# Two-layer decoder trunk: value products by fours, layer 0's first rows normed two by two, one product of its end moved back

## The reference

```python
for i in range(2):
    x = x + mixer_i(rms_norm(x, norm_i)) @ w_out_i
return rms_norm(x, final_norm)

# mixer 0: sliding window of 128, 4 key/value groups, partial rope, a sink logit per head
q, k, v, gate = split(h @ w_in)
o = banded_attention(rope(q), rope(k), v, 127, sinks);   return o * silu(gate)

# mixer 1: three patterns (window, dilation) = (128,1), (512,4), (2048,16), each with own q, k, v
for gi: o_gi, lse_gi = banded_attention on every dil-th row
w = softmax over gi of lse_gi;   return sum(w_gi * o_gi) * silu(gate)
```

## Time and profile before

| | us |
|---|---|
| median of 3 runs | 1302.64 (1300.87 to 1304.35) |
| profiled execution, its own time | 1303.58 |
| its span | 1301.8 |
| granted TensorE clock, mean | 0.995 |
| PE busy | 1261.5 (97%) |
| PE weight load busy | 1184.5 (91%) |
| DVE busy | 768.7 (59%) |
| ACT busy | 644.3 (49%) |
| POOL busy | 370.1 (28%) |

### The profile page before, as it was taken

One profiled execution on the slowest core, in us unless ns is written; L12 is line 12 of the kernel. 1 busy time (PEld: TensorE's weight loads), 2 busy tenths in 40 slices (PEclk: granted clock), 3 DMA queues, 4 the chain that ended last, 5 costly groups with the idle time before them and its releaser, 6 DMA issues.

```text
span 1301.8 us, 24575 instructions
## 1 busy us (share of the span) xinstructions
PE 1261.5 (97%) x8714; PEld 1184.5 (91%) x8714; DVE 768.7 (59%) x2339; ACT 644.3 (49%) x1777; POOL 370.1 (28%) x427
## 2 busy tenths in 40 slices
PE   4999999999899999999999999999999999999997
PEld 4999998988799999999989999999999899987997
DVE  5745453555662545666646776556765566768925
ACT  6445463545741445554546555446554456546312
POOL 2312151240401022212212942215922217710110
PEclk9999999999999999999999999999999999999999
DMA  5101022031546211110121321202211212314723
GB/s 203 35 24 50 26 60 79 18 98 49 159 151 202 96 27 54 39 27 19 33 74 50 92 67 27 74 26 67 84 58 36 65 38 80 92 36 127 223 98 129
DMA packets 101223, 97.29 MB, mean 75 GB/s; under 512 B 30704, under 2 KB 87536, under 8 KB 101104
## 3 DMA queue, kind: packets, MB, share of 16 engines
q1 hardware_dynamic: 101104, 95.73, 24.6%
HBM read 79.46 MB, written 16.25 MB: 74 GB/s over the span
## 4 chain that ended last, share of the span: by engine, by line
PE 80%; issue 5%; DVE 4%; DMA 4%; POOL 3%; ACT 2%; SPq 1%; DVEq 0%; POOLq 0%; ACTq 0%
PE j_bank L1196 56%; PE o_bank L1339 6%; PE t_bank L1318 5%; PE s_bank L1305 4%; PE j_bank L1283 3%; PE s_bank L1307 2%; POOL xr L1129 1%; DMA w_raw<-in_w_qkv 1%; DMA coef<-coef_dram 1%; PE o_bank L1196 1%; PE t_bank L1196 1%; DMA gate<-in_positions 1%; PE s_bank L1196 1%; DVE xr L1843 1%; POOL xr L1136 1%
## 5 line engine op out<-in xcount | busy, mean ns | idle before, releaser
L1196 PE MATMUL j_bank<-w_hi,ht_hi 128*128 128x384 f32 (+1 forms) x1312 | 445.0, 339 | 4.2 <-ACT v L1452 2.4
L1196 PE MATMUL j_bank<-w_lo,ht_hi 128*128 128x384 f32 (+1 forms) x1312 | 432.9, 330 | 0.0
L1196 PE MATMUL j_bank<-w_hi,ht_lo 128*128 128x384 f32 (+1 forms) x1312 | 432.8, 330 | 0.0
L1196 PEld LDWEIGHTS j_bank<-w_hi,ht_hi 128*128 128x128 f32 x1312 | 248.5, 189 | 15.0 <-issue 7.9
L1438 ACT ACTIVATE probs<-probs,stat 128x256 f32<-128x256 f32 (+1 forms) x512 | 231.1, 453 | 58.8 <-DVE stat L1697 56.8
L1090 POOL TENSOR_TENSOR w_lo<-w_raw,w_hi 128x768 fp32r<-128x768 f32 (+1 forms) x60 | 104.2, 1736 | 543.6 <-ACT w_hi L1429 444.0
L1196 PEld LDWEIGHTS j_bank<-w_lo,ht_hi 128*128 128x128 f32 x1312 | 248.8, 190 | 0.0
L1196 PEld LDWEIGHTS j_bank<-w_hi,ht_lo 128*128 128x128 f32 x1312 | 248.4, 189 | 0.0
L1429 ACT ACTIVATE w_hi<-w_raw 128x768 fp32r<-128x768 f32 (+1 forms) x120 | 88.4, 763 | 83.3 <-PE j_bank L1196 43.6
L826 ACT COPY probs_t<-t_bank 128x256 f32<-128x256 f32 (+1 forms) x84 | 39.0, 464 | 167.5 <-PE o_bank L1339 162.0
L1689 DVE CUSTOM_DVE_ANT_0 probs<-s_bank,masks 128x256 f32<-128x256 f32 x224 | 85.9, 420 | 47.5 <-PE t_bank L1318 46.7
(11 more groups left out here) (176 smaller groups left out, 1902.6 us busy)
## 6 DMA issues: line engine op xcount, KB each, us to landing
w_raw<-in_w_qkv SPq DMA_DIRECT2D x64, 384.0 KB, 3.5
coef<-coef_dram SPq DMA_DIRECT2D x96, 128.0 KB, 3.0
w_raw<-in_w_gate SPq DMA_DIRECT2D x32, 256.0 KB, 3.3
mix_dram<-xr SPq DMA_DIRECT2D x12, 512.0 KB, 3.9
w_raw<-in_w_out SPq DMA_DIRECT2D x16, 384.0 KB, 3.8
qk<-mix_dram SPq DMA_DIRECT2D x12, 512.0 KB, 5.7
xr<-in_x SPq DMA_DIRECT2D x8, 512.0 KB, 7.9
out<-xr SPq DMA_DIRECT2D x7, 512.0 KB, 2.7
```

Of the source, the lines that this page charges most:

```text
L1196: last = pe.matmul(to, a(x_, kt), b(y_, kt), start=(start and kt == kts[0] and x_ == y_), stop=(stop and kt == kts[-1] and x_ == 1))
```

## The change

**1. More value products by fours.** `by_fours` now is asked of a unit: all of layer 0; in layer 1 patterns 1 and 2, the first step, and units 12 to 15 of pattern 0. The turns of the third and fourth unit are copied into row 0 of a result region that is said to be free (`turned_at`): region 3 in layer 0 (1 in its last step), (t+2) % 4 in layer 1. Before these copies the copying engine waits for the region (`guard_region`): in pattern 1 for all of the group before to be mixed, in pattern 0 for its r = 0 half, in layer 0's last step for the stores of a mix.

**2. Layer 0's first four rows.** ACT squares all four. Rows 0 and 1 get their own inverse roots and are scaled whole by DVE, rows 2 and 3 follow, scaled in column halves (DVE left, ACT right). PE transposes rows 0 and 1 as they are ready into eight banks, one for each kt, and 2 and 3 behind them (`norm_first`). The pieces of blocks 0 and 1 then both run on the column groups kt 0 to 3 before either runs on 4 to 7. The transposes of rows 4 to 7 stand one block later. The rope's angles are begun ahead of the roots, the rest of the rope and the constants are spread over blocks k = 2 to 4. Positions come on ACT's queue and the small loads have semaphores of their own.

**3. End of layer 0.** `end_product(last, 0, 0)` moves on DVE from before `empty_turn(last, 15)` to the fifth of the mix splits, behind a weight's lo copy.

```diff
@@ -143,7 +143,7 @@
-NORM_BEHIND = {1: (0, 1, 2), 2: (3, 4, 5), 3: (6, 7)}
+NORM_BEHIND = [{2: (0, 1, 2, 3), 3: (4, 5, 6, 7)}, {1: (0, 1, 2), 2: (3, 4, 5), 3: (6, 7)}]
 FILLS_BEFORE = {10: ("Q0", 0), 12: ("Q1", 0), 14: ("K", 0)}
@@ -228,22 +228,41 @@
-def by_fours(s):
-    return s.p == 2 if s.layer == 1 else not s.last
+def by_fours(s, u):
+    return s.layer == 0 or s.p > 0 or s.first or u >= 12
 def values_at(s, a):
     b, u = unit_before(s, a, V_BACK)
-    if b is None or (by_fours(b) and u % 4 == 0):
+    if b is None or (by_fours(b, u) and u % 4 == 0):
         return []
-    return [(b, n) for n in range(u - 2 if by_fours(b) else u, u + 2)]
-def own_place(s, u):
-    return u // 2 % 2 if by_fours(s) and s.layer == 1 else 1
+    return [(b, n) for n in range(u - 2 if by_fours(b, u) else u, u + 2)]
+def turned_at(s, u):
+    if s.layer == 1 and s.p == 2:
+        return None, u % 2, u // 2 % 2
+    if not by_fours(s, u) or u % 4 < 2:
+        return None, u % 2, 1
+    return (1 if s.last else 3) if s.layer == 0 else (s.t + 2) % 4, u % 2, 1
+TURNED_AFTER = {}
+_user = {}
+for _s in STEPS:
+    for _u in range(UNITS):
+        _region, _place, _own = turned_at(_s, _u)
+        _halves = [(_region, _place, _own)] + ([(_region, _place, 0)] if _s.has_prev(_u % NB) else [])
+        TURNED_AFTER[_s.t, _u] = max(_user.get(_h, -1) for _h in _halves) + 1
+        for _h in _halves:
+            _user[_h] = UNITS * _s.t + _u
@@ -799,9 +828,22 @@
         def turned_place(s, u):
-            if by_fours(s) and s.layer == 0 and u % 4 >= 2:
-                return ot[GROUPS - 1][:, 0, :].rearrange("p (a b c) -> p a b c", a=2, b=4)[:, u % 2, :, :]
-            return probs_t[:, u % 2, :, :]
+            region, place, _ = turned_at(s, u)
+            if region is None:
+                return probs_t[:, place, :, :]
+            return ot[region][:, 0, :].rearrange("p (a b c) -> p a b c", a=2, b=4)[:, place, :, :]
+        def guard_region(eng, s):
+            if s.layer == 0:
+                if s.last:
+                    eng.wait_ge(mix_out, 64)
+            elif s.p == 1:
+                eng.wait_ge(mixed, mix_links_before(s.t))
+            elif not s.first:
+                eng.wait_ge(mixed, mix_links_before(s.t - 1) + mix_links(STEPS[s.t - 1], (0,)))
         def store_turn(eng, copy, s, u):
@@ -809,21 +851,16 @@
             i = UNITS * s.t + u
             key = (s.t, u)
 ...
-                if i >= 4:
-                    eng.wait_ge(summed, i - 3)
-            elif by_fours(s) and u >= 2:
-                eng.wait_ge(summed, UNITS * s.t + u - 3)
-            elif i >= 2:
-                eng.wait_ge(summed, i - 1)
 ...
+            if turned_at(s, u)[0] is not None:
+                guard_region(eng, s)
+            if TURNED_AFTER[key] > 0:
+                eng.wait_ge(summed, TURNED_AFTER[key])
             src = t_bank[TURN.bank(key)][:, :].rearrange("p (j e q) -> p j e q", j=2, e=2)
 ...
+            def norm_first():
+                for b, e in ((0, "v"), (1, "v")):
+                    pe.wait_ge(xn_done[e], b + 1)
+                    for kt in range(KT):
+                        pe.transpose(first_bank[kt][:, b * P:(b + 1) * P], xr[:, b, kt * P:(kt + 1) * P], ident[:, :])
+                for kt in range(KT):
+                    if kt == 0:
+                        pe.wait_ge(xn_done["v"], 3)
+                    if kt == 4:
+                        pe.wait_ge(xn_done["a"], 1)
+                    for b in (2, 3):
+                        last = pe.transpose(first_bank[kt][:, b * P:(b + 1) * P], xr[:, b, kt * P:(kt + 1) * P], ident[:, :])
+                    last.then_inc(norm_full, 1)
             def products(to, a, b, kts, start, stop):
@@ -1351,11 +1403,9 @@
                 pe.transpose(to, comb[:, 1 - s.layer, rows], ident[:, :]).then_inc(turned, 1)
             pe.wait_ge(consts, 1)
-            for kt in range(6):
-                norm_piece(0, kt, 0)
+            norm_first()
             piece(("qkv", 0, 0), (0,))
-            for kt in range(6, KT):
-                norm_piece(0, kt, 0)
@@ -1363,8 +1413,8 @@
                         if item[0] == "fill":
                             fill(*item[1:])
                         else:
-                            piece(item[1:], (1,) if layer == 0 and k == 0 else (0, 1))
-                    for kt in NORM_BEHIND.get(k, ()):
+                            piece(item[1:], (1,) if layer == 0 and k < 2 else (0, 1))
+                    for kt in NORM_BEHIND[layer].get(k, ()):
 ...
+            def square_first(n):
+                act.wait_ge(x_in[n], 16)
+                if n > 0:
+                    act.wait_ge(squared["va"[n % 2]], (n + 1) // 2)
+                act.activation(square_a, xr[:, n, :], ACT.Square, accum_out=sums[:, n:n + 1]).then_inc(squared["av"[n % 2]], 1)
+            act.wait_ge(const_link, 3)
+            act.activation(sums[:, NB:NB + 1], no_sink[:, 0:1], ACT.Sqrt, scale=0.0)
+            square_first(0)
+            square_first(1)
+            act.wait_ge(first_v, 1)
+            act.activation(ssq[:, 1, 0:2], ssq[:, 0, 0:2], ACT.Sqrt).then_inc(first_a, 1)
+            square_first(2)
+            square_first(3)
+            act.wait_ge(norm_v, 1)
+            act.activation(ssq[:, 1, 2:4], ssq[:, 0, 2:4], ACT.Sqrt).then_inc(norm_a, 1)
+            w_hi([(0, 0), (0, 1)])
+            act.wait_ge(norm_v, NORM_LINKS)
+            for n in (2, 3):
+                last = act.activation(xr[:, n, 512:], xr[:, n, 512:], ACT.Copy, scale=ssq[:, 2, n:n + 1])
+            last.then_inc(xn_done["a"], 1)
             for kt in range(KT):
                 empty_norm(0, kt, 0)
-                if kt == 3 or kt == 5:
-                    w_hi([(0, 2 if kt == 3 else 3)])
-            norm_half(0, 1)
+                if kt == 4:
+                    w_hi([(0, 2), (0, 3)])
+            square(0, 4)
+            square(0, 6)
+            empty_piece(("qkv", 0, 0))
+            root(0, 1)
+            scale_rows(0, 1)
             w_hi(splits_of("start, next job"))
@@ -2000,30 +2079,45 @@
                 link(dve.tensor_scalar(cos_to[:, :, HALF_ROT:ROT], halves, -2.0, 1.0, ALU.mult, ALU.add), rope_v, ROPE_LINKS + 2)
                 dve.sem_inc(tables, 1)
-            norm_half(0, 0)
+            angles()
+            less_turns(0, 2 * np.pi * 256)
+            dve.wait_ge(squared["a"], 1)
+            dve.wait_ge(squared["v"], 1)
+            inverse(0, slice(0, 2), first_v, first_a)
+            for n in (0, 1):
+                dve.tensor_scalar(xr[:, n, :], xr[:, n, :], ssq[:, 2, n:n + 1], None, ALU.mult).then_inc(xn_done["v"], 1)
+            dve.wait_ge(squared["a"], 2)
+            dve.wait_ge(squared["v"], 2)
+            inverse(0, slice(2, 4))
+            for n in (2, 3):
+                last = dve.tensor_scalar(xr[:, n, 0:512], xr[:, n, 0:512], ssq[:, 2, n:n + 1], None, ALU.mult)
+            last.then_inc(xn_done["v"], 1)
             w_lo(splits_of("start"))
             for kt in range(KT):
                 empty_norm(0, kt, 0)
-                if kt == 3:
+                if kt == 4:
 ...
                     w_lo(splits_of("start, second half"))
             norm_half(0, 1)
+            empty_piece(("qkv", 0, 1))
             w_lo(splits_of("start, next job"))
             for layer in (0, 1):
                 steps = LAYER_STEPS[layer]
                 for k in range(NB):
                     if layer == 0 and k == 2:
-                        rope_angles()
+                        less_turns(1, 2 * np.pi)
+                        within_half_turn()
+                    if layer == 0 and k == 3:
+                        rope_tables()
                     if layer == 0 and k == 4:
-                        rope_tables()
                         constants()
                     if k == NB - 1:
                         w_lo([(JOB["qkv", steps[1].t], 2), (JOB["qkv", steps[1].t], 3)])
                     for item in start_work(steps[0], k):
                         if item[0] == "fill":
                             fill_lo(*item[1:])
-                        else:
@@ -2069,7 +2163,8 @@
                                 coef_copy(s, 0)
                 last = steps[-1]
                 coefs_first(last, 1)
-                end_product(last, 0, 0)
+                if layer == 1:
+                    end_product(last, 0, 0)
                 empty_turn(last, UNITS - 1)
                 store_ot(last, 1, 1)
 ...
                     if k == 4:
                         w_lo(END_SPLIT[layer])
+                        if layer == 0:
+                            end_product(last, 0, 0)
                         end_mix(last, 0)
                 for k in range(2):
                     mix_split(layer, MIX_LOADS + k, ot[out_region(last)][:, k, :])
```

(6 more changed lines are left out.)

103 lines of the change are left out of this document (51 added, 52 removed).

## The result

The changed kernel takes 1310.41 us (median of 4 runs, 1309.24 to 1312.53), the kernel before beside it 1302.59 (4 runs). The ratio is 1.0062, 95% interval 1.0042 to 1.0081: slower by 7.8 us, forecast was 9.1. The profiled execution took 1311.19, its span is 1309.4.

What follows compares the result with a forecast made beforehand. PE's queue was taken to bound the kernel (busy 1261.5 of 1301.8 us). Terms -6.7 - 6.8 - 6.6 + 22.3 + 6.9 = +9.1 on the median 1302.64 gave 1311.7 us, range 1303 to 1319.

Steps and rivals of the forecast that it cites:

- Part 2: Layer 0's end: moving the end product removes PE's wait on DVE's copy and the half clock, -6.8 us.
- Part 1: The start: first rows transposed earlier and scaling halved, so first pieces and fill come sooner, -6.7 us.
- Part 3: Value groups of four in place of two: 20 outside the stalls save 0.33 us each, -6.6 us.
- Parts 4 and 5: Steps 8, 11, 14: new waits for POOL's mix cost +22.3 us, PE's half clock behind them +6.9.
- A: Rival: the guards cost nothing because POOL finishes before the copies come; 1280.5 us, chance 0.08.
- B: Rival: the stalls are there, but PE keeps its clock or regains it at once; 1304.8 us, chance 0.08.
- C: Rival: ACT and DVE leave each guard with owed work, PE's next turn waits 4 us again; 1324, chance 0.07.
- D: Rival: the start's gain is lost to other waits, +5 to +6.7 us, 1316 to 1318; chance 0.05.

Runs made afterwards that it cites:

- The end product alone: The kernel before with only layer 0's end product moved on DVE: 1294.76 us, ratio 0.9947.
- against twos: The changed kernel with pattern 1 (steps 5, 8, 11, 14) having value products by twos again below unit 12: 1288.95 us, ratio 0.9897.
- With twos: The light guard with mended start, but layer 0's last step has values by twos again below unit 12: 1288.28 us, run again 1286.81.
- 58 transposes: The changed kernel with 58 useless PE transposes ahead of the waiting turn in steps 8, 11 and 14: 1305.52 us, ratio 1.0033.
- light guard: The changed kernel, but in steps 8, 11 and 14 copies wait only for the mix's r = 0 half: 1288.37 us, ratio 0.9898.
- 40 of them: The changed kernel with 40 useless PE transposes ahead of the waiting turn in steps 8, 11 and 14: 1308.99 us, ratio 1.0061.
- light guard with mended start: The light guard, plus POOL's quarter 1 weight copy waiting for DVE's quarter 0 and ACT's quarters 2 and 3 split: 1284.43 us, again 1285.11.

## Why the prediction was right, point by point

The time (1311.7 forecast, 1310.4 measured), the sign and the mechanism held. By its own parts:

**Part 2, layer 0's end, held**: -6.8 forecast, -6.87 measured, from the row at 354.30. The end product alone gives -6.3, the later rows have no new wait. The 32 value products run from 349.17 and the coefficient turn comes 5.13 behind, where I had 5.3, and the clock over 348 to 354 is 1.00.

**Part 1, the start, was 2.3 too hopeful**: -6.7 forecast, -4.4 measured, below its lower bound of 4.9. Rows of the changed kernel, PE:

```profile
30.00 1.04 PE L1224 MATMUL s_bank<-ident,xr 128*128 128x128 f32 x8
...
36.35 1.32 PE L1224 MATMUL s_bank<-ident,xr 128*128 128x128 f32 x8 [0.25 <-DVE ht_lo L1812]
...
38.74 0.42 PE L1248 MATMUL j_bank<-w_hi,ht_hi 128*128 128x384 f32 x1
...
47.78 1.03 PE L1335 MATMUL t_bank<-ident,qk 128*128 128x128 f32 x8
```

Two terms failed. The two pieces end at 30.00 - 4.15 = 25.85 in place of 25.0. I let ACT's hi copies of the second weights cost 2 x 0.83 and never asked when those weights land; they wait for the lo copies of the first, and that chain (DVE's 2.57, the DMA, ACT's 1.41) set the end. The second term is the transposes of rows 4 to 7. I priced the waits that go, but not that four kt in a row must now find empty banks: the second four take 38.74 - 36.35 = 2.39, the first four 1.67. From the pieces' end to the first fill PE needs 21.93, before it was 52.17 - 29.88 - 1.83 = 20.46, so 1.5 went there.

**Part 3, merged groups, held in price where no wait is near, and failed in one cover.** Eight groups in s4-7 give 2.9, 0.36 each, where I had 0.33. In steps 8, 11 and 14 the price does not hold in full: nine groups gave 0.2 against twos, in place of 3.0. In layer 0's last step the same edit costs 0.5 (-0.4 and +0.9) in place of a gain of 1.0. ACT and PE there, after:

```profile
320.97 1.28 ACT L1545 ACT_TABLE_LOAD   x1
322.27 1.92 ACT L1545 ACTIVATE gate<-gate 128x2048 f32<-128x2048 f32 x1
...
324.67 1.28 ACT L1490 ACT_TABLE_LOAD   x1
325.97 0.40 ACT L1490 ACTIVATE probs<-probs,stat 128x128 f32<-128x128 f32 x1
...
326.99 0.41 PE L1370 MATMUL t_bank<-ident,probs 128*128 128x128 f32 x2 [0.64 <-ACT probs L1490]
327.98 0.63 PE L1370 MATMUL t_bank<-ident,probs 128*128 128x128 f32 x4 [0.57 <-ACT probs L1490]
```

ACT needs 5 us for the silu with its two table loads before it can make the exponentials. The value block of 1.09 in this pair covered it, and merging moved that block a pair later. With twos the waits vanish. I costed the edit at its own saving and didn't name the work that PE's block had been covering.

**Parts 4 and 5, the stalls.** For the three stretches the parts sum to 22.3 + 6.9 less nine merged groups outside the stalls (3.0) = 26.2; measured 20.9. Steps 11 and 14 hold: (7.1 or 6.8) + 2.3 - 1.0 = 8.4 and 8.1 forecast, 8.5 and 7.4 measured. The stall's anatomy too: PE's waits are 5.88, 6.68 and 5.71, 18.3 of the 21.0 at the top of the page, where 7 to 8 each was said. From POOL's end at 741.47 to the piece at 748.70 are 7.2, where 5.4 + 2.3 = 7.7 was said, and with the clock held up 5.6 to 5.9, where 5.4 was said. Step 8 was over-priced by 4.7: 9.7 against 5.0. Its step was the row 757.49, taken as where POOL always is. POOL's first mix of that group, before and then after:

```profile
710.16 1.30 POOL L1129 TENSOR_TENSOR xr<-xr,coef 128x512 f32<-128x512 f32 x1 [5.38 <-DMA coef<-coef_dram]
```

```profile
694.30 1.31 POOL L1165 TENSOR_TENSOR xr<-xr,coef 128x512 f32<-128x512 f32 x1 [3.23 <-DMA coef<-coef_dram]
```

Counted from the coefficient turn (701.60, 687.89) that is 8.56 and 6.41 us. The coefficients go to DRAM and come back, and this round trip was 2.2 us late in the one execution that I had read. The same distance for the three groups in all 14 profiled executions is 6.2 to 7.6 in 39 of the 42 cases and 8.0 to 8.6 in three. The mix that starts late ends late: from the coefficient turn to POOL's last multiply were 55.89 (757.49) and 52.10 (739.99), 3.8 less. Of this 2.2 is the round trip, and 0.97 is a second wait of POOL for coefficients, at 754.40 before, which the changed kernel's execution hadn't. It hadn't a wait of PE for POOL either, of 0.88 at 739.24 before, and the stall itself was 0.5 shorter than said. The three make 5.2, 0.5 more than the 4.7 to be explained; where that 0.5 went I can't say. The clock, 2.3 for each stall by my row at layer 0's end and 6.9 in all, is 1.4, 1.8 and 2.7, 5.8 in all, by the run with 58 transposes. The half rate fell on 3.6, 4.6 and 6.4 us of PE's work behind the three stalls.

**Why the net was so near.** Measured less forecast, by stretches: start +2.3, last step +1.5, end -0.1, the eight groups -0.3, step 8 -4.7, steps 11 and 14 +0.1 and -0.7, rest +0.4: -1.5 in all. Two gains that were too hopeful and one loss that was too large cancel; the nearness of 1311.7 to 1310.4 is luck to that extent, the sign is not.

**The rivals.** A, guards that cost nothing, is what the light guard gives: I said 1280.5, measured 1288.4. In the stretches of its profiled execution 18.1 of the 22.1 came. The start missed 2.4, the last step 1.5 and the fifteen groups of steps 8, 11 and 14 1.6 (3.3 in place of 4.95); layer 0's end and s4-7 gave 1.2 and 0.4 more. The rest of the 7.9 isn't in the stretches: this execution was 2.9 faster than the median of its runs, and that of the kernel before 0.9 slower. B, a clock that doesn't fall, is what the run with 58 transposes made: 1305.5, with 1304.8 said; left alone it does fall. C, a second stall behind each guard, isn't there: behind the turn that it stood for (744.34 in step 8) PE waits only once, 0.33, 0.32 and 0.33 us in the three steps, and then for nothing for 30 us or more. D is true in part: 2.3 of the start's 6.7 were lost, where it had 5 to 6.7.

The rule of the Trainium skill, "SBUF — State Buffer", section "SBUF: two separate sides", on the shared port, which I weighed and left out, gave at most 1.0 us in the stalls. In step 11 the add that took 2.11 took 1.48 in the changed kernel, at 932.28, while DVE stood, and in step 14 it went from 1.85 to 1.48. With the light guard, where DVE doesn't stand, the same adds took 2.12, 1.52 and 1.84 in steps 8, 11 and 14, in the changed kernel 1.49, 1.48 and 1.48. So such a gain was there, in most executions, and leaving them out was a small error.

## What to carry to other kernels

A wait on "all of the group before" where only a half of it is read can cost more than everything else that a change gains: ask of each new guard which item of the other engine's queue it really needs, and lay its end against the start of the first instruction behind the guard. A stretch of work that is moved away was also a cover; look what the other engines finish beneath it. And a time that hangs on a DMA round trip must be read from more than one place of the trace before it is used as a term.

## What the runs showed of the hardware

- A DVE lo copy of 128x768 from two SBUF inputs, begun 0.34 us behind POOL's copy of the same size, took 2.57 us in place of 0.95, and with POOL's moved behind it 0.95. This is what the Trainium skill, "SBUF — State Buffer", section "SBUF: two separate sides", says of a VectorE operation with two SBUF inputs against a GpSimd one: the first to start keeps the shared ports for its whole length, the other is blocked. It also met a one-input DVE operation of the rope, where I hadn't expected it: 30.97 for 1.89 us in place of 0.26, while POOL's copy ran from 30.87 for 1.87.
- PE kept its higher clock with 58 transposes in the stall and lost it with 40 of them, behind which it stood 2.1 to 2.6 us. After stalls of 5.7 to 6.7 us it did 3.6 to 6.4 us of work at half clock. Nothing finer was tried.
- The same kernel's profiled executions differ by 5 us over the stretches of steps 8 to 14 (light guard with mended start: -4.4 in one, +0.5 in the other). 2.8 of it lie in step 8's, where the coefficients came 2.2 later in the second and PE waited 1.24 and 0.88 us for POOL (at 721.76 and 723.96); for the rest no run gives a reason.
